# Expert routing inside the attention stage, a ring of eleven weight pieces, and rows added where they belong: a hybrid encoder layer on one core

## Chip, core and metric

The kernel runs on one core of a Trainium2 chip. The metric is the device time of one execution in microseconds, the median over several runs. The kernel before took 1273.96 us (three runs: 1273.96, 1270.16, 1274.58).

## What is computed

One encoder layer is applied to two sequences of 512 tokens of width 1024 that share all weights. The parts after the token mixer are what matters here:

```python
x = x + mix
x = x + memory_cross_attention(rms_norm(x, norm_xa), rms_norm(mem, norm_mem), w_xq, w_xkv, xq_norm, xk_norm, w_xo)
x = x + hier_moe(rms_norm(x, norm_ffn), w_router_group, b_router_group, w_router_expert, b_router_expert,
                 w_e_gate, w_e_up, w_e_down)
...
# hier_moe, for each of the 1024 tokens:
g_sel = argmax(g_logits)                  # 1 of 4 groups, gate = max of the softmax
top_val, top_loc = top_k(e_logits[g_sel], 2)   # 2 of the 8 experts in that group
gates = softmax(top_val) * g_gate
y = sum over the two experts of gate * ((silu(x @ w_e_gate[e]) * (x @ w_e_up[e])) @ w_e_down[e])
```

There are 32 experts; one has 3 MiB of float32 weights (gate and up 1024x256 each, down 256x1024). A block of work is one expert with up to 128 of its tokens. 1024 tokens with two experts each are 64 tokens per expert on average.

## The kernel before

**Arithmetic.** Each float32 product is made from three fast ones (`three`, L832 to L838): ScalarE copies a float32 tile to a rounded high part (L1263), VectorE subtracts it from the original to get the low part (L1992 for expert weights, L1985 for token rows), and TensorE adds high x high, high x low and low x high.

**Stages.** A table of steps (`timeline`, L61) sets one order in which every engine walks through the mixer and the cross-attention. The cross-attention part runs over eight tiles of 128 tokens (L124 to L143); a tile's last step is its router product (`router`), of which VectorE keeps only the logits (L1862). Engines wait for each other by semaphores alone; each executes its own list in order.

**Routing.** After the last router product VectorE makes the choice for all 1024 tokens at once (L1877 to L1960): maxima, one-hot masks, ranks inside an expert (TensorE sums, L1144), slots, and the list of token numbers per expert (`ids`, sixteen small products at L1155). TensorE has nothing else to do there. Meanwhile SyncE loads weights, and ScalarE and GpSimd prepare expert 0 (GpSimd makes its low parts, L2222).

**Experts.** The 32 experts run in a software pipeline (`pipeline`, a hardware loop over pairs). Six buffers `eraw` of 512 KB hold raw pieces of one expert; high and low parts go to further double buffers. For expert n, TensorE transposes the gathered rows of expert n+1 (L1169), makes gate and up for n, then the down product of n-1. GpSimd gathers the rows of expert n+2 from `ffn_rows` by an indirect DMA (L2236, behind a tiny `anchor` operation, L2235), and stores the 128 result rows of expert n-1 to `expert_rows` (L2245). SyncE reloads a raw piece when its low part is made (L806). An indirect DMA skips the list's empty places.

**Combine.** When all 32 are stored, GpSimd fetches for each token tile the two result rows per token (sixteen indirect DMAs, L2288), VectorE adds them with their gates to `x_sb` (L2064), and SyncE writes the outputs (L828). Experts with more than 128 tokens would take `further` blocks; none occurs with these inputs.

Of the kernel before, what the change touches and what calls it, by code (L numbers as in the profile page):

```python
# [17 lines left out]
I32 = mybir.dt.int32  # L18
# [28 lines left out]
NB = NE + NO  # L47
# [4 lines left out]
N_RAW = 2  # L52
N_BANKS = 8
N_FIRST = 2
N_CONST = 8
N_INIT = 8
ROUND = 2.0 ** 23
R_STAGES = 5


def timeline():  # L61
# [62 lines left out]
    for i in range(-2, NT + 2):  # L124
# [38 lines left out]
def bank_uses(step):  # L163

    kind = step[0]
    if kind == "conv" or kind in ("vc", "vt", "dtp", "z", "mv", "hn1", "dt", "sback", "sout", "router", "dtt", "out"):
        return 1
# [108 lines left out]
def encoder_layer(nc, dram, out):  # L276
# [3 lines left out]
    with ctx:  # L280
# [3 lines left out]
        bank = [ctx.enter_context(nc.psum_tensor(f"bank{b}", [P, 512], F32)) for b in range(N_BANKS)]  # L284
# [5 lines left out]
        y_dram = nc.dram_tensor("expert_rows", (NE * P, D), F32).ap()  # L290
        yo_dram = nc.dram_tensor("further_rows", (NO * P, D), F32).ap()


        x_sb = ctx.enter_context(nc.sbuf_tensor("x_sb", [P, NT, D], F32))
        ident = ctx.enter_context(nc.sbuf_tensor("ident", [P, P], F32))
        logits = ctx.enter_context(nc.sbuf_tensor("logits", [P, NT, NG + NE], F32))
        stk = ExitStack()
        ctx.enter_context(stk)

        def sb(name, shape, dt=F32):  # L300
            return stk.enter_context(nc.sbuf_tensor(name, shape, dt))
# [109 lines left out]
        router_w = sb("router_ws", [P, KT, NG + NE])  # L411
        sb("apart", [P, 320])
# [6 lines left out]
        router_b = sb("router_b", [P, NG + NE])  # L419
        stk.close()  # L420
        NORMED = {"mix": (xn, gain), "mem": (xn, gain), "xa": (xn, gain), "ffn": (xn_ffn, gain_ffn)}


        def se(name, shape, dt=F32):
            return ctx.enter_context(nc.sbuf_tensor(name, shape, dt))

        WgH = [se(f"WgH{i}", [P, KT, 2 * DE], F32R) for i in range(2)]
        WgL = [se(f"WgL{i}", [P, KT, 2 * DE], F32R) for i in range(2)]
        WdH = [se(f"WdH{i}", [P, 2, D], F32R) for i in range(2)]
        WdL = [se(f"WdL{i}", [P, 2, D], F32R) for i in range(2)]  # L430
        eraw = [se(f"eraw{j}", [P, 1024]) for j in range(6)]
        xg = [se(f"xg{i}", [P, D]) for i in range(2)]
        xgH = [se(f"xgH{i}", [P, KT, P], F32R) for i in range(2)]
        xgL = [se(f"xgL{i}", [P, KT, P], F32R) for i in range(2)]
        eth = se("eth", [P, DE])
        ehb = se("ehb", [P, DE])
        hbH = se("hbH", [P, 2, P], F32R)
        hbL = se("hbL", [P, 2, P], F32R)
        ey = [se(f"ey{i}", [P, D]) for i in range(2)]
        idc = [se(f"idc{i}", [P, 1], U32) for i in range(2)]  # L440

        iota_e = se("iota_e", [P, NB + 1])
        iota_p = se("iota_p", [P, P])
        token0 = se("token0", [P, NT])
        token1 = se("token1", [P, NT])
        anchor = se("anchor", [P, 1])
        r_g = se("r_g", [P, NT, NG])
        r_g2 = se("r_g2", [P, NT, NG])
        r_e = se("r_e", [P, NT, NE])
        r_eq = se("r_eq", [P, NT, NE])  # L450
        oh = se("oh", [P, 2, NT, NE])
        r_max = se("r_max", [P, 3, NT])
        r_idx = se("r_idx", [P, 3, NT])
        gates = se("gates", [P, 2, NT])
        r_t = se("r_t", [P, 4, NT])
        cnt_b = se("cnt_b", [P, NT, NE], BF16)
# [1904 lines left out]
```

## Time and profile before

| | us |
|---|---|
| median of three runs | 1273.96 |
| span of the profiled execution | 1272.4 |
| last router logits on VectorE | 835.8 |
| first gate/up product of an expert | 887.2 |
| last down product ends | 1221.5 |
| busy: TensorE / VectorE / ScalarE / GpSimd | 1028.0 / 838.4 / 525.7 / 263.0 |

The time of an execution has its span in it and what lies around the span; the profiled execution's own time is not given beside its span, and the median of the runs is 1.6 us above that span. The span falls into a long part under the step table (to 836 us), routing (to 887), the experts (to 1221) and the combine. A timeline row gives start, duration, engine, line, operation and output<-inputs; where it is marked x4, four like instructions in a row are merged.

### The profile page before, as it was taken

The page shows a single profiled execution, that of the slowest core. Times are in us where ns is not written, and L with a number is a line of the kernel's source. Part 1 is how long each engine was busy: PE and PEld are TensorE (multiplying, and loading weights), DVE is VectorE, ACT ScalarE, POOL GpSimd, SP SyncE. Part 2 cuts the span into 40 slices and gives each one's busy share as a digit, 9 for nine tenths or more (in the row PEclk, how much of TensorE's full clock was granted, in tenths as well). Part 3 has the DMA queues.
Part 4 walks back from the last instruction along what each step waited for, and adds up shares of the span by engine and source line. Part 5 has one row for each costly group of instructions (what it writes and reads, how often), then busy time and mean ns, then how long its engine had stood idle before and what let it go on. Part 6 is the DMA issues. An engine that isn't in the chain of part 4 may idle for free. (4 is left out here: it accounts for less than half of the span.)

```text
span 1272.4 us, 15688 instructions
## 1 busy us (share of the span) xinstructions
PE 1028.0 (81%) x5076; PEld 833.5 (66%) x5076; DVE 838.4 (66%) x1295; ACT 525.7 (41%) x944; POOL 263.0 (21%) x364
## 2 busy tenths in 40 slices
PE   1878979988897989899969999822899989999930
PEld 1656757766675768778758788722777777777720
DVE  4425856876675586752445554376899999999934
ACT  3222243323234333321233333231677777777710
POOL 1204304321431331100101111142111111111123
PEclk9989988878898888889979999755999999999975
DMA  5131214122122313424210000053799999999948
GB/s 183 36 97 61 91 67 126 30 72 75 59 91 69 131 59 111 138 80 143 72 50 1 34 17 34 33 180 130 261 382 371 373 373 383 389 363 370 351 139 306
DMA packets 75800, 201.41 MB, mean 158 GB/s; under 512 B 13088, under 2 KB 19648, under 8 KB 75744
## 3 DMA queue, kind: packets, MB, share of 16 engines
q1 hardware_dynamic: 58240, 151.15, 33.5%
q0 software_dynamic: 15808, 47.89, 10.4%
q10 hardware_dynamic: 1696, 1.65, 0.4%
q8 instruction: 32, 0.52, 0.2%
q14 instruction: 24, 0.20, 0.1%
HBM read 177.58 MB, written 31.46 MB: 164 GB/s over the span
## 5 line engine op out<-in xcount | busy, mean ns | idle before, releaser
L836 PE MATMUL bank<-Wh,hTh 128*128 128x512 f32 x384 | 162.0, 422 | 4.6 <-issue 4.6
L837 PE MATMUL bank<-Wl,hTh 128*128 128x512 f32 x384 | 156.8, 408 | 0.0
L838 PE MATMUL bank<-Wh,hTl 128*128 128x512 f32 x384 | 156.1, 407 | 0.0
L1992 DVE TENSOR_TENSOR WgL<-eraw,WgH 128x1024 fp32r<-128x1024 f32 x124 | 143.5, 1216 | 0.6 <-ACT WgH L1263 0.5
L1263 ACT ACTIVATE WgH<-eraw 128x1024 fp32r<-128x1024 f32 x128 | 127.0, 1064 | 12.1 <-DMA eraw<-w_e_up 8.5
L836 PE MATMUL bank<-WgH,xgH 128*128 128x512 f32 x256 | 103.6, 405 | 0.0
L1580 DVE TENSOR_TENSOR Wl<-raw,Wh 128x1024 fp32r<-128x1024 f32 (+1 forms) x64 | 77.3, 1216 | 37.9 <-ACT Wh L1263 37.7
L837 PE MATMUL bank<-WgL,xgH 128*128 128x512 f32 x256 | 100.9, 394 | 0.0
L838 PE MATMUL bank<-WgH,xgL 128*128 128x512 f32 x256 | 100.5, 393 | 0.0
L836 PEld LDWEIGHTS bank<-Wh,hTh 128*128 128x128 f32 x384 | 77.6, 202 | 22.4 <-issue 6.6
L838 PEld LDWEIGHTS bank<-Wh,hTl 128*128 128x128 f32 x384 | 76.3, 199 | 17.3
L837 PEld LDWEIGHTS bank<-Wl,hTh 128*128 128x128 f32 x384 | 77.2, 201 | 15.7
L836 PE MATMUL bank<-hTh,Wh 128*128 128x512 f32 (+1 forms) x176 | 74.3, 422 | 9.2 <-issue 8.3
L1992 DVE TENSOR_TENSOR WdL<-eraw,WdH 128x1024 fp32r<-128x1024 f32 x62 | 73.2, 1220 | 6.7 <-ACT WdH L1263 6.4
L1263 ACT ACTIVATE Wh<-raw 128x1024 fp32r<-128x1024 f32 (+1 forms) x64 | 63.1, 999 | 30.4 <-PE bank L838 19.6
L1263 ACT ACTIVATE WdH<-eraw 128x1024 fp32r<-128x1024 f32 x64 | 64.5, 1050 | 25.3 <-PE bank L838 22.1
L886 PE MATMUL bank<-ident,xn 128*128 128x128 f32 x160 | 31.2, 359 | 52.6 <-DVE xn L1589 52.6
L837 PE MATMUL bank<-hTl,Wh 128*128 128x512 f32 (+1 forms) x176 | 72.7, 413 | 0.0
L838 PE MATMUL bank<-hTh,Wl 128*128 128x512 f32 (+1 forms) x176 | 72.4, 411 | 0.0
L2245 POOL DMA_DIRECT2D expert_rows<-ey x32 | 18.7, 583 | 214.8 <-DVE ey L2016 198.8
L886 PEld LDWEIGHTS bank<-ident,xn 128*128 128x128 f32 x160 | 25.1, 186 | 57.0 <-DVE xn L1589 38.0
L1413 ACT ACTIVATE dec<-dec,ncs 128x128 f32<-128x128 f32 x128 | 38.6, 388 | 45.2 <-DVE dec L1774 45.2
(314 smaller groups left out, 2261.7 us busy)
## 6 DMA issues: line engine op xcount, KB each, us to landing
eraw<-w_e_gate SPq DMA_DIRECT2D x64, 512.0 KB, 6.0
eraw<-w_e_up SPq DMA_DIRECT2D x64, 512.0 KB, 6.5
eraw<-w_e_down SPq DMA_DIRECT2D x64, 512.0 KB, 6.4
raw<-w_in SPq DMA_DIRECT2D x72, 256.0 KB, 2.9
expert_rows<-ey POOLq DMA_DIRECT2D x32, 512.0 KB, 6.4
raw<-w_xkv SPq DMA_DIRECT2D x16, 256.0 KB, 3.0
raw<-w_out SPq DMA_DIRECT2D x16, 256.0 KB, 3.4
raw<-mix_scratch SPq DMA_DIRECT2D x16, 256.0 KB, 3.2
```

Of the source, the lines that this page charges most:

```text
L836: pe.matmul(dst, ah, bh, start=first, stop=False)
L837: pe.matmul(dst, ah, bl, start=False, stop=False)
L838: return pe.matmul(dst, al, bh, start=False, stop=last)
L886: last = pe.transpose(b[:, j * P:(j + 1) * P], NORMED[st][0][:, f * P:(f + 1) * P], ident[:, :])
L1263: return act.activation(dst, src, ACT.Copy, **kw)
L1413: last = act.activation(dec[:, dr, h, :], dec[:, dr, h, :], ACT.Exp, bias=ncs[:, dr, c, h:h + 1])
L1580: tt(lo, src, h, ALU.subtract).then_inc(w_low, 1)
L1992: tt(lo, as_piece(eraw[j], j), h.bitcast(F32), ALU.subtract).then_inc(ew_low, 1)
L2245: pool.dma_start(rows_, ey[i][:, :]).then_inc(ey_st[i], 16)
```

## The change

**Per-tile routing.** Two steps `rank` and `slots` join the table, and the `router` step does the whole choice for its own tile with the eight-largest operations of VectorE. After the last tile only one product (`place`) is left before the token numbers are known. The gates are computed later, beside the first expert.

**Weights.** Eleven buffers of 1 MiB each (three pieces per expert) are laid over memory that the attention stage gives back. The low part is written in place over the raw piece; high parts have three buffers for gate/up and two for down. SyncE issues the first eleven loads from the last attention tiles on, and each further one when TensorE has used the piece. The hardware loops are gone: all 32 experts are written out.

**Rows.** ScalarE stores `x` of each tile to `partial_rows` during attention. For each expert GpSimd gathers the token rows and the partial rows; VectorE adds gate times result to the partial rows; GpSimd scatters them by three indirect DMAs, to `partial_rows` for a token's first expert and to `y_prompt` or `y_sample` for its second (places that do not belong to a target are out of range and skipped). Experts of the four groups alternate, so that neighbours share no token. There is no combine.

**Low parts.** GpSimd makes half of the down piece's low part, a sixth of an expert's.

```diff
     for i in range(-2, NT + 2):
...
+        tl += on(i - 2, ("rank", i - 2), ("slots", i - 2))
...
+        if i == NT:
+            tl.append(("pre",))
...
-    return tl
+    return tl + [("place",)]
...
+                    link(dve.max(gm8[:, i, :], logits[:, i, 0:8]))
+                    link(dve.max_index(gi8[:, i, :], gm8[:, i, :], logits[:, i, 0:8]))
+                    link(dve.tensor_copy(r_ix[:, 0:1], gi8[:, i, 0:1]))
+                    link(ts(r_pen[:, :], iota_e[:, 0:NG], r_ix[:, 0:1], NEG, ALU.not_equal, ALU.mult))
...
+            wait_full(sp, ("hn1", "xq", NT - 1))
+            for q in range(3 * NE):
+                n, j = divmod(q, 3)
...
+                elif q >= N_EW:
+                    m, i = divmod(q - N_EW, 3)
+                    if i < 2:
+                        sp.wait_ge(g_used, 2 * m + i + 1)
+                    else:
+                        sp.wait_ge(d_used, m + 1)
+                load_piece(expert(n), j, q % N_EW, eraw_ld[q % N_EW])
...
+            def gather_rows(n):
+                e = expert(n)
+                if n > 2:
+                    pool.wait_ge(xg_full, 2 * n - 4)
+                fetch(xg[n % 3][:, :], hn_dram, idh[:, e:e + 1], last_row).then_inc(xg_ld[n % 3], 16)
...
+            def store_rows(n):
+                e = expert(n)
+                pool.wait_ge(ey_done, n + 1)
+                done, rows_ = out_st[n % 4], pg[n % 4][:, :]
+                spread_rows(out[0][0], idp[:, e:e + 1], rows_, last_half).then_inc(done, 16)
+                spread_rows(out[1][0], ids[:, e:e + 1], rows_, last_half).then_inc(done, 16)
+                spread_rows(px_dram, idf[:, e:e + 1], rows_, last_row).then_inc(done, 16)
+
+            def down_low(n):
+                k = piece(n, 2)[0]
+                pool.wait_ge(dhi_done, n + 1)
+                pool.tensor_tensor(elo[k][:, D:2 * D], eraw[k][:, D:2 * D], dhi[n % 2][:, 1, :].bitcast(F32),
+                                   ALU.subtract).then_inc(dlo_p, 1)
...
+            for n in range(1, NE):
+                if n > 1:
+                    store_rows(n - 2)
+                if n + 1 < NE:
+                    gather_sums(n + 1)
+                if n + 3 < NE:
+                    gather_rows(n + 3)
+                if n + 1 < NE:
+                    down_low(n + 1)
...
+            def add_rows(n):
+                e = expert(n)
+                dve.wait_ge(d_used, n + 1)
+                dve.wait_ge(pg_ld[n % 4], 16 * (n // 4 + 1))
+                stt(pg[n % 4][:, :], y_ps[:, :], gate_s[:, e:e + 1], pg[n % 4][:, :], ALU.mult, ALU.add)\
+                    .then_inc(ey_done, 1)
...
-            for i in range(NT):
-                for c in range(2):
-                    dve.wait_ge(yg_ld[i % 2][c], 16 * (i // 2 + 1))
-                    stt(x_sb[:, i, :], yg[i % 2][c][:, :], gates[:, c, i:i + 1], x_sb[:, i, :], ALU.mult, ALU.add)\
```

The first place is VectorE in a middle tile of cross-attention. `xn` is the normalised input of a later tile, which TensorE transposes as soon as it is there. Before:

```order
L1862 TENSOR_TENSOR logits<-bank,router_b 128x36
L1589 SCALAR_TENSOR_TENSOR xn<-x_sb,rs,gain 128x1024
L1825 COPY probT<-bank 128x512
L1597 TENSOR_TENSOR hTl<-bank,hTh 128x4x128 x2
L1640 TENSOR_SCALAR xqT<-bank,cols 128x512
```

Now (`eix`, `oh`, `cnt_b` and `idv` are the tile's expert numbers, one-hot masks, counts and token values):

```order
L1989 TENSOR_TENSOR logits<-bank,router_b 128x40
L1991 MAX gm<-logits 128x8
L1992 MAX_INDEX gi<-gm,logits 128x8
L1993 CAST r_ix<-gi 128x1
L1994 TENSOR_SCALAR r_pen<-iota_e,r_ix 128x4
L1995 TENSOR_TENSOR r_e<-logits,r_pen 128x32
L1997 MAX em<-r_e 128x8
L1998 MAX_INDEX ei<-em,r_e 128x8
L1999 CAST eix<-ei 128x2
L2001 TENSOR_SCALAR oh<-iota_e,eix 128x32 x2
L2003 TENSOR_TENSOR cnt_b<-oh 128x32
L2006 TENSOR_TENSOR csum<-csum,cnt_b 128x32
```

Behind these come two more (L2008, `idv`), and only then `xn` (now L1710): fourteen instructions stand between the logits and `xn` where there was none.

The second place is GpSimd among the experts. Before, one expert in the loop is:

```order
L2235 TENSOR_TENSOR anchor<-token 128x1
L2236 DMA xg<-ffn_rows,idc 128x1024
L2243 REGISTER_ALU
L2245 ISA
L2245 DMA expert_rows<-ey 128x1024
```

Now one expert is (`pg` holds partial rows, `elo` the low part over the raw piece):

```order
L2382 DMA y_prompt<-pg_86,idp 512x1024
L2382 DMA y_sample<-pg_86,ids 512x1024
L2382 DMA partial_rows<-pg_86,idf 1024x1024
L2377 DMA pg_89<-partial_rows,idh 128x1024
L2377 DMA xg_85<-ffn_rows,idh 128x1024
L2408 TENSOR_TENSOR elo_63<-eraw_52,dhi_78 128x1024
```

One indirect and one plain DMA have become five indirect ones and an operation on 128x1024 elements.

The third place is VectorE among the experts, one expert of the new order:

```order
L2065 TENSOR_TENSOR hbL<-hb_ps,hbH 128x256
L2046 TENSOR_TENSOR xgL_82<-xg_ps,xgH_80 128x512 x2
L1684 TENSOR_TENSOR elo_72<-eraw_61,ghi_74 128x2048
L1684 TENSOR_TENSOR elo_73<-eraw_62,ghi_75 128x2048
L2059 SCALAR_TENSOR_TENSOR ehb<-eth,gu_ps 128x256
L2061 TENSOR_TENSOR ehb<-ehb,gu_ps 128x256
L2072 SCALAR_TENSOR_TENSOR pg_87<-y_ps,gate_s,pg_87 128x1024
L2052 TENSOR_TENSOR elo_63<-eraw_52,dhi_78 128x1024
```

Six low parts of 1024 columns have become two of 2048 and one of 1024, and the copy of half a result has become an addition over 1024 columns.

## Rows read from the trace of the kernel before

**Rows 1.** Stretches: us, busy PE, PEld, DVE, ACT, POOL (instructions), clock, DMA, GB/s.

```profile
722.00:744.00 22.00, 20.34 (x122) 17.52 (x121) 11.73 (x19) 7.96 (x19) 3.69 (x8) 1.00 0.06 25
...
840.00:880.00 40.00, 2.15 (x32) 1.83 (x32) 33.98 (x59) 12.23 (x13) 19.25 (x10) 0.50 0.52 174
...
960.00:1200.00 240.00, 224.55 (x1061) 182.87 (x1060) 226.19 (x299) 185.00 (x252) 41.73 (x69) 0.99 0.99 375
```

**Rows 2.** Timeline around logits and normalised inputs, tiles 3 and 7 of attention.

```profile
703.59 1.28 DVE L1589 SCALAR_TENSOR_TENSOR xn<-x_sb,rs,gain 128x1024 f32<-128x1024 f32 x1
...
704.92 1.97 PE L886 MATMUL bank<-ident,xn 128*128 128x128 f32 x8 [0.54 <-DVE xn L1589]
...
827.68 0.20 DVE L1862 TENSOR_TENSOR logits<-bank,router_b 128x36 f32<-128x36 f32 x1 [3.40 <-PE bank L1134]
...
829.13 1.97 PE L886 MATMUL bank<-ident,xn_ffn 128*128 128x128 f32 x8 [1.56 <-DVE xn_ffn L1589]
```

**Rows 3.** Timeline from the last logits to the first expert product.

```profile
835.84 0.19 DVE L1862 TENSOR_TENSOR logits<-bank,router_b 128x36 f32<-128x36 f32 x1 [6.78 <-PE bank L1134]
...
846.05 0.17 DVE L1911 TENSOR_SCALAR r_t<-r_t 128x8 f32<-128x8 f32 x1
846.25 0.17 DVE L1912 TENSOR_TENSOR r_t<-r_t 128x8 f32<-128x8 f32 x1
...
870.45 0.82 PE L1155 MATMUL bank<-oneh_b,oneh_p 128*128 128x48 f16 x16 [23.05 <-DVE oneh_b L1954]
...
887.21 0.77 PE L836 MATMUL bank<-WgH,xgH 128*128 128x512 f32 x1
```

**Rows 4.** Groups of instructions, 960 to 1200 us (23 experts).

```profile
L1992 DVE TENSOR_TENSOR WgL<-eraw,WgH 128x1024 fp32r<-128x1024 f32 x92 | 106.4, 1216 | 0.6 <-ACT WgH L1263 0.5
...
L1985 DVE TENSOR_TENSOR xgL<-bank,xgH 128x512 fp32r<-128x512 f32 x46 | 29.4, 679 | 0.1
...
L2236 POOL DMA_INDIRECT xg<-ffn_rows,idc x23 | 24.1, 1048 | 10.8 <-issue 10.8
...
L2001 DVE TENSOR_TENSOR ehb<-ehb,bank 128x256 f32<-128x256 f32 x23 | 9.7, 421 | 0.8
```

**Rows 5.** DMA view, 960 to 1200 us; the second row ends in us to landing.

```profile
DMA packets 26470, 89.95 MB, mean 375 GB/s; under 512 B 4513, under 2 KB 4513, under 8 KB 26470
...
xg<-ffn_rows,idc POOLq DMA_INDIRECT x23, 7.0
```

**Rows 6.** Timeline: down products of the first and last expert, and the combine.

```profile
904.04 0.39 PE L838 MATMUL bank<-WdH,hbL 128*128 128x512 f32 x1
...
1221.09 0.39 PE L838 MATMUL bank<-WdH,hbL 128*128 128x512 f32 x1
...
1230.24 1.03 POOL L2288 DMA_INDIRECT eraw<-expert_rows,slot  x1 [0.30 <-issue]
1231.58 0.99 POOL L2288 DMA_INDIRECT eraw<-expert_rows,slot  x1 [0.30 <-issue]
```

**Rows 7.** Timeline: GpSimd and VectorE side by side, routing and first experts.

```profile
846.34 9.26 POOL L2222 TENSOR_TENSOR WgL<-eraw,WgH 128x1024 fp32r<-128x1024 f32 x4 [7.90 <-ACT WgH L1263]
...
848.76 2.27 DVE L1915 TENSOR_TENSOR gates<-gates,r_t 128x8 f32<-128x8 f32 x1
...
871.92 4.63 DVE L1992 TENSOR_TENSOR WgL<-eraw,WgH 128x1024 fp32r<-128x1024 f32 x4
872.03 1.16 POOL L2235 TENSOR_TENSOR anchor<-token 128x1 f32<-128x1 f32 x1 [11.82 <-DVE idc L1979]
873.36 1.91 POOL L2236 DMA_INDIRECT xg<-ffn_rows,idc  x1 [0.17 <-POOL anchor L2235]
...
992.90 0.18 POOL L2235 TENSOR_TENSOR anchor<-token 128x1 f32<-128x1 f32 x1 [1.65 <-DVE idc L1979]
993.55 1.05 POOL L2236 DMA_INDIRECT xg<-ffn_rows,idc  x1 [0.47 <-issue]
994.11 4.62 DVE L1992 TENSOR_TENSOR WgL<-eraw,WgH 128x1024 fp32r<-128x1024 f32 x4
```

More of the change, by code:

```diff
@@ L421, in encoder_layer @@
+        oh = nc.alloc_sbuf_tensor_at("oh", [P, 2, NT, NE], F32, offset=at["y1"] + 2048)
         NORMED = {"mix": (xn, gain), "mem": (xn, gain), "xa": (xn, gain), "ffn": (xn_ffn, gain_ffn)}
[L424 to L429, printed above, removed]
@@ new lines, in encoder_layer, with sw @@
+        xg = [se("xg0", [P, D], "Wl1", 2 * K4), se("xg1", [P, D], "Wl1", 3 * K4), se("xg2", [P, D], "xn", 4 * K4)]
+        pg = [se(f"pg{i}", [P, D], "xn", K4 * i) for i in range(4)]
+        small = [at["xkT"] + 6 * K4]
+        def sw(name, shape, dt=F32):
+            t = nc.alloc_sbuf_tensor_at(name, shape, dt, offset=small[0])
+            small[0] += -(-int(np.prod(shape[1:])) * 4 // 32) * 32
+            assert small[0] <= at["router_b"]
+            return t
+        eth = sw("eth", [P, DE])
@@ new lines, in encoder_layer, with expert, piece, fill @@
+        out_st = [sem(f"out_st{i}") for i in range(4)]
+        o_v = sem("o_v")
+        o_pe = sem("o_pe")
+        f_id = sem("f_id")
+        f_row = sem("f_row")
+        anchored = sem("anchored")
+        f_ld = [sem(f"f_ld{j}") for j in range(3)]
+        f_v = sem("f_v")
+        f_a = sem("f_a")
+        f_pe = sem("f_pe")
+        def expert(n):
+            return n % NG * EPG + n // NG
+        def piece(n, j):
+            return (3 * n + j) % N_EW, (3 * n + j) // N_EW
+        def fill(n, j):
+            k, turn = piece(n, j)
+            two = sum(x % 3 < 2 for x in range(k, 3 * n + j + 1, N_EW))
+            return eraw_ld[k], 16 * (turn + 1 + two)
@@ L829, in _ @@
-            sp.wait_ge(out_st, 16 * NT)
+                sp.wait_ge(d_used, b + NE)
+                for j in range(3):
+                    load_piece(e, j, j, f_ld[j])
+            further(sp, more, more_first)
         @block.tensor
@@ L1226, in _ @@
-            further(pe, more)
+                last.then_inc(d_used, 1)
+            turn_rows(0)
+            gate_up(0)
+            turn_rows(1)
+            pe.wait_ge(vals_done, 1)
+            for j in range(2 * NT):
+                pe.matmul(r_ps[:, 0:3 * NE].rearrange("p (a b) -> p a b", a=3), oneh_p[:, j, :], idv2[:, j, :, :],
+                          start=j == 0, stop=j == 2 * NT - 1)
+            pe.matmul(r_ps[:, 3 * NE:4 * NE], ones_b[:, :], csum[:, NT, :], start=True, stop=True).then_inc(vals_full, 1)
@@ L1229, in _ @@
+            further(pe, more, more_first)
         @block.scalar
@@ L1522, in _ @@
+            further(act, more, more_first)
         @block.vector
@@ new lines, in _ @@
+            gate_low(0, 1)
+            down_low(0)
+            gate_values()
+            rows_low(0)
+            gate_low(1, 0)
+            hidden(0)
+            rows_low(1)
+            gate_low(1, 1)
+            down_low(1)
+            slot_values()
+            for n in range(1, NE):
+                hidden_low(n - 1)
+                if n + 1 < NE:
+                    rows_low(n + 1)
+                    gate_low(n + 1, 0)
+                    gate_low(n + 1, 1)
+                hidden(n)
+                add_rows(n - 1)
+                if n + 1 < NE:
+                    down_low(n + 1)
+                if n == 2:
+                    counts()
```

973 lines of the change are left out of this document (528 added, 445 removed).

## The prediction
> **What bounds the kernel now.** I read the stretches first [rows 1]. In a tile of cross-attention TensorE is busy 20.3 of 22 us at full clock and VectorE 11.7, so TensorE sets the pace there. From 840 to 880 us TensorE works 2.2 of 40 us: this is routing. Among the experts three things are close to full at once: TensorE 224.6, VectorE 226.2 of 240 us, and the DMA engines at a share of 0.99. The DMA view gives 89.95 MB for 23 experts, 3.91 MB each, at 375 GB/s [rows 5], which is 10.4 us per expert. The timelines fix the stages: last logits at 835.8, first expert product at 887.2 [rows 3], first down product ended at 904.4, last at 1221.5 [rows 6]. So the 31 experts between take 10.23 us each, and 50.9 us follow them up to the span of 1272.4 us. GpSimd is nearly free among the experts: 41.7 us in 240.
>
> **The change, part by part.** All sums run against the span of 1272.4 us; the median of the runs is 1.6 us above it.
>
> *Routing inside attention.* A small dependent VectorE operation follows the one before after 0.20 to 0.21 us [rows 3]. Fourteen of them now stand between a tile's logits and `xn`: 14 x 0.21 = 2.9 us. Before, `xn` began right at the logits, and TensorE already waited for it (0.54 us) [rows 2]. So this is no free time on VectorE: TensorE stands still 2.9 us more in each of the four tiles that still prepare a later one, 11.6 us. In the next two tiles the chain holds up the copy of `probT`; there about half of it shows, 3 us together. Behind the seventh tile's logits stand the chain, the rank product and four operations of `slots`, in front of the last `xn_ffn`, for which TensorE waits [rows 2]: 2.9 + 0.5 + 1.0 = 4.4 us. `slots` also stands ahead of `xn_ffn` in the other tiles, 0 to 1.0 us each; I take 0.6, 3.5 us for six. The small products of `rank` and a clock that may sag with more gaps: 0 to 8 us, I take 3.5. Sum 26 us (bounds 12 and 34), so the last logits come at 862. The forms `MAX` and `MAX_INDEX` are not in this trace; between the smallest operation, 0.17, and one on 256 columns, 0.42 [rows 3, 4], I take the small one, since they read 8 to 40 columns. The stores of `x` by ScalarE and the early weight loads cost nothing: DMA is 0.06 busy there [rows 1].
>
> *From the last logits to the first expert product* it takes 51.4 us now [rows 3]. After the change: the chain 2.9, rank and slots 1.5, sixteen placing products 2.0 (the present ones took 0.82 in half the precision [rows 3]), token numbers 0.5. From `anchor` at 872.0 to the first product at 887.2 were 15.2 us [rows 7, 3]; without `anchor` and the second tile's transposes ahead of the product I take 12. Sum 19 us: the first expert product starts at 881, 6 us earlier only. The first down product ends 17.2 us after that before; now its neighbour's gate/up waits for low parts that TensorE's own use releases, about 3 us more. So it ends at 901 instead of 904.
>
> *An expert in the steady state.* TensorE keeps its work, 224.6/23 = 9.8 us. VectorE: two low parts of 2048 columns and one of 1024 are 5 units of 1.16 us (the step of four in 4.62 [rows 7]), 5.8; token rows 2 x 0.64, three hidden operations of 0.42 [rows 4], the addition 1.3: 9.6 us, from 9.8 now. The DMA volume stays: one full store of 128 rows was as much as a gather and a scatter of 64. The eleven pieces loaded ahead give the queue a lead of about one expert. These three would give 10.3 to 10.7 us per expert.
>
> GpSimd is the new candidate. Two indirect DMAs in a row start 1.34 us apart [rows 6]; five per expert are 6.7. A subtraction over 1024 columns takes 2.31 (9.26 for four [rows 7]). With 0.1 for waits that is 9.1 us in a list that has to be done in order. And it does not get them undisturbed. At 872.0 `anchor` took 1.16 us beside the low parts of VectorE, where it takes 0.18 at 992.9; the indirect DMA behind it took 1.91 instead of 1.05; and VectorE's 8-column product of the gates took 2.27 us beside GpSimd's subtractions [rows 7]. So a GpSimd instruction waits for the running two-input operation of VectorE to end, and the other way round. At 993.6 the indirect DMA had begun before the low parts, and neither suffered: it needs the port only at its start. Hence the wait per GpSimd instruction: the port is VectorE's for 5.8 us of an expert, in pieces of 2.3, 2.3 and 1.2, so an arrival in it waits 1.0 us on average. At a pace T the chance of that is 5.8/T, six arrivals per expert: T = 9.1 + 6 x 5.8/T, which is 12.0 us. An instruction that was just served leaves 1.2 us in which it needs no port, so I take a little less: **T = 11.7**. Its ends: 10.3, where the waits fall on nothing, and 14.9, where GpSimd makes no progress in all of the 5.8 us. An indirect DMA that scatters is not in the trace; between a plain store's 0.58 us of issue and the 1.91 of a hindered gather I take the gather's 1.34.
>
> In return VectorE waits for GpSimd's 2.31 us operation, for none of it or all. The two ask for the port when the same high part is ready, and VectorE has other operations to do in part of that time, so I take a third, 0.8 us: VectorE needs 10.4 us, inside the 10.3 to 10.7.
>
> The Trainium skill, "Perfetto Trace Analysis", section "Optimizing Scalar/DVE Operations", speaks against this part of the change: since GpSimd and VectorE share a read port, moving work between the two might not help. Taken to its end it would give VectorE 9.6 + 2.3 = 11.9 us per expert in place of 10.4; the rows at 848.8 and 872.0 show the port waits it speaks of, and not how much of them lies beside other work.
>
> *Sum.* GpSimd runs up to two experts ahead at the start. Its gather for expert 5 is issued at about 914 (the down product of expert 0 at 901, its addition, three scatters, two gathers with their waits). From there 26 experts at T to the gather of the last one. Behind that: subtraction 3.3, two shorter rounds of 9.1 without the token gather, then the last three result sets at 3 x 1.34 = 4 us each, 12; landing 5.5 (gathers take 7.0 in a full queue [rows 5]) and 2 for the ends of all engines, with 1.3 for the addition: 42 us. 914 + 26 x 11.7 + 42 = 1260, and 1.6 for what lies around: **1262 us**. What the combine cost, 50.9 us, is mostly gained; the slower experts take most of it back.
>
> **Rivals.**
>
> *A, the forecast*: GpSimd sets the pace, T from 11.2 to 12.2: 1249 to 1275. For it speak the two port rows; against it, that the order of arrivals can lock into a phase with few waits. Chance 0.50.
>
> *B, GpSimd keeps up*: then TensorE, VectorE and DMA hold 10.5 us: 901 + 31 x 10.5 + 13 (addition, scatters, landing, end) + 1.6 = 1241; with 10.3 to 10.7, and attention up to 12 us quicker, 1223 to 1248. It needs waits under 1.5 us per expert. Chance 0.30.
>
> *C, slower than before*: the same mechanism, but arrivals fall at the start of the wide operations, as at 872.0, where the two instructions waited 0.98 and 0.9 us of pieces of 1.16. With pieces twice as wide, two such arrivals per expert wait 1.9 us each, even if the other four wait for nothing: T = 9.1 + 3.8 = 12.9, and 914 + 26 x 12.9 + 42 + 1.6 = 1293. It decides from T = 12.4 on. It also comes about if a scatter costs 0.4 us more than a gather. Chance 0.17.
>
> *D, GpSimd is shut out wholly*: its pace is 9.1 + 5.8 = 14.9, the time 1345 us. The gather at 993.6 that ran on in 1.05 us beside four low parts speaks against it; 0.03. The page "SBUF — State Buffer" of the Trainium skill, section "SBUF: two separate sides", says that GpSimd cannot write the descriptors of its DMAs while VectorE is in an operation that takes both ports. If a two-input subtraction counted as such a one, this case would be the rule.
>
> **How the numbers follow.** A measurement of this kernel can tell 0.5% from no change, 6.4 us: faster is below 1267.6, slower above 1280.3. A lies below 1267.6 in 6 of 10, between in 3.5: 0.30 and 0.17, the rest 0.03 above. B is faster, 0.30. C and D are slower, 0.20. Faster 0.60, same 0.17, slower 0.23. The range takes in A, the upper two thirds of B and C: 1225 to 1293. The likeliest case's own range is 1249 to 1275.
>
> **What would show it.** Last logits near 862 and TensorE's wait for `xn` near 3.5 us instead of 0.54; first expert product near 881. Among the experts: GpSimd without idle time except its port waits, indirect DMAs longer than 1.05 us on average (near 1.5), TensorE waiting for `xg`, DMA share near 0.85. If instead indirect DMAs are near 1.05 and GpSimd waits for VectorE's additions, B holds. If the last logits stay near 836, my first term is wrong, and the time is 26 us lower in every case.

## The result, and the profile after

The changed kernel takes **1293.09 us** (median of 4 runs, 1290.03 to 1294.7), the kernel before 1272.06 us beside it (1269.9 to 1274.58). The ratio is 1.0167, with a 95% interval of 1.0147 to 1.0186: slower by 1.7%. The forecast was 1262 us, faster. The profiled execution took 1290.03 us, with a span of 1288.2.

The stretches of the changed kernel, to be laid beside [rows 1] (same columns):

```profile
722.00:744.00 22.00, 17.42 (x97) 15.35 (x96) 12.85 (x35) 5.51 (x13) 3.31 (x7) 0.84 0.11 44
840.00:880.00 40.00, 19.94 (x100) 17.31 (x98) 24.35 (x70) 12.03 (x14) 14.51 (x18) 0.61 0.34 119
960.00:1200.00 240.00, 206.46 (x892) 167.14 (x891) 199.60 (x173) 141.45 (x135) 212.95 (x116) 0.92 0.88 320
```

In attention TensorE does less in the same time, at a lower granted clock (0.84, where it had 1.00; among the traced kernels with this attention code, 0.77 to 0.92 in that window). Among the experts TensorE and VectorE have both become less busy, and GpSimd went from 41.7 to 213 of 240 us. What its six instructions per expert cost is in the groups of that stretch (mean ns; then the idle time ahead of them and its releasers):

```profile
L2382 POOL DMA_INDIRECT y_prompt<-pg,idp x20 | 53.9, 2696 | 3.3 <-issue 3.2
L2408 POOL TENSOR_TENSOR elo<-eraw,dhi 128x1024 fp32r<-128x1024 f32 x20 | 50.5, 2527 | 0.5
L2382 POOL DMA_INDIRECT y_sample<-pg,ids x19 | 37.7, 1985 | 5.8 <-issue 5.8
L2377 POOL DMA_INDIRECT pg<-partial_rows,idh x19 | 25.5, 1341 | 5.8 <-issue 5.8
L2382 POOL DMA_INDIRECT partial_rows<-pg,idf x19 | 23.6, 1239 | 5.8 <-issue 5.8
L2377 POOL DMA_INDIRECT xg<-ffn_rows,idh x19 | 22.3, 1176 | 5.8 <-issue 4.3 <-PE xg_ps L1222 1.5
```

The six means add up to 10.96 us, and the issue gaps (0.3 us ahead of an indirect DMA, 0.17 behind the subtraction) bring them to 12.4. Of the idle time only 1.5 us in 240 are a wait for another engine: GpSimd's list is full. TensorE in its turn waits for the row gathers that GpSimd issues, as the longest waits of the same stretch show (in total, times, longest):

```profile
ACT dhi L1354 <- PE y_ps L897: 44.1, 18, 2.5
PEld xg_ps L1222 <- DMA xg<-ffn_rows,idh: 21.5, 16, 2.7
DVE elo L1684 <- ACT ghi L1354: 19.5, 26, 1.7
PEld hb_ps L1247 <- DVE ehb L2061: 18.5, 10, 2.9
PE xg_ps L1222 <- DMA xg<-ffn_rows,idh: 18.5, 16, 2.5
```

**Where the time went**, by the end of the twelve down products of the first and of the last expert. Now they end at 903.9 and 1275.2 us, before at 904.4 and 1221.5 [rows 6]. The way to the first is 0.5 us shorter. The 31 experts between take 11.98 us each instead of 10.23: 54.3 us more. Behind the last it takes 13.0 us to the span's end instead of 50.9: 38.0 less. Together -0.5 + 54.3 - 38.0 = +15.8, the difference of the spans (1288.2 - 1272.4). So scattering partial rows did save the closing combine, and slower experts took more than that back.

One round of GpSimd (POOL) and of VectorE (DVE) shows how. These are rows of the timeline of the changed kernel: start, duration, then in brackets the idle time ahead.

```profile
1045.90 2.42 POOL L2408 TENSOR_TENSOR elo<-eraw,dhi 128x1024 fp32r<-128x1024 f32 x1
1048.48 2.88 POOL L2382 DMA_INDIRECT y_prompt<-pg,idp  x1 [0.17 <-issue]
1051.67 2.39 POOL L2382 DMA_INDIRECT y_sample<-pg,ids  x1 [0.30 <-issue]
1054.37 0.98 POOL L2382 DMA_INDIRECT partial_rows<-pg,idf  x1 [0.31 <-issue]
1055.65 1.03 POOL L2377 DMA_INDIRECT pg<-partial_rows,idh  x1 [0.30 <-issue]
1056.99 1.56 POOL L2377 DMA_INDIRECT xg<-ffn_rows,idh  x1 [0.31 <-PE xg_ps L1222]
1058.57 2.42 POOL L2408 TENSOR_TENSOR elo<-eraw,dhi 128x1024 fp32r<-128x1024 f32 x1
1061.15 2.88 POOL L2382 DMA_INDIRECT y_prompt<-pg,idp  x1 [0.17 <-issue]
```

```profile
1047.75 2.72 DVE L1684 TENSOR_TENSOR elo<-eraw,ghi 128x2048 fp32r<-128x2048 f32 x1 [1.11 <-ACT ghi L1354]
1050.90 2.29 DVE L1684 TENSOR_TENSOR elo<-eraw,ghi 128x2048 fp32r<-128x2048 f32 x1 [0.42 <-ACT ghi L1354]
...
1056.43 1.23 DVE L2052 TENSOR_TENSOR elo<-eraw,dhi 128x1024 fp32r<-128x1024 f32 x1 [0.72 <-ACT dhi L1354]
...
1059.66 5.69 DVE L1684 TENSOR_TENSOR elo<-eraw,ghi 128x2048 fp32r<-128x2048 f32 x2 [0.47 <-ACT ghi L1354]
```

VectorE's first wide low part (2048 columns) begins in the last half microsecond of GpSimd's subtraction, and waits for its end (2.72 us, where the next takes 2.29). The scatter to `y_prompt` then meets that operation from its start and ends 0.89 us after it (1051.36 against 1050.47). The scatter to `y_sample` starts 0.8 us into the second and ends 0.87 us after it. The row gather meets the low part of 1024 columns and ends 0.89 us after that. The two that fall between, at 1054.37 and 1055.65, take 0.98 and 1.03. The next subtraction ends at 1060.99. VectorE's next wide operation was ready at 1059.66 and is held until then (the two records together last 5.69 us, where twice 2.29 is 4.6), and the next `y_prompt` takes 2.88 us again.

That is what keeps the two lists in step. In 17 of the 19 rounds from 960 to 1200 us a wide operation becomes ready while the subtraction runs, 0.4 to 2.5 us before its end. It is held to that end, and `y_prompt`, which starts 0.17 us behind the subtraction, meets it at its start: 2.88 us each time. In the other two rounds no wide operation becomes ready in that time, and `y_prompt` takes 1.02 us.

### The profile page after: what moved, and what is told of

Same layout as the page of the kernel before. It is cut to its first block and busy times, and to the rows that moved or that the text cites. A ratio compares the mean times of both kernels' runs of the same rounds, so it can differ in the third digit from the quotient of the medians.

```text
span 1288.2 us, 14286 instructions
## 1 busy us (share of the span) xinstructions
PE 1065.4 (83%) x5093; PEld 863.5 (67%) x5093; DVE 842.8 (65%) x1285; ACT 501.3 (39%) x816; POOL 519.3 (40%) x445
## 5 line engine op out<-in xcount | busy, mean ns | idle before, releaser
L1684 DVE TENSOR_TENSOR elo<-eraw,ghi 128x2048 fp32r<-128x2048 f32 x64 | 173.0, 2727 | 26.5 <-ACT ghi L1354 25.7
L1354 ACT ACTIVATE ghi<-eraw 128x2048 fp32r<-128x2048 f32 x64 | 121.7, 1918 | 21.6 <-PE gu_ps L897 19.5
L895 PE MATMUL gu_ps<-ghi,xgH 128*128 128x512 f32 x256 | 111.8, 437 | 5.7 <-DVE xgL L2046 5.7
L896 PE MATMUL gu_ps<-elo,xgH 128*128 128x512 f32 x256 | 106.3, 415 | 0.0
L897 PE MATMUL gu_ps<-ghi,xgL 128*128 128x512 f32 x256 | 105.5, 412 | 0.0
L1354 ACT ACTIVATE dhi<-eraw 128x2048 fp32r<-128x2048 f32 x32 | 61.2, 1912 | 75.6 <-PE y_ps L897 73.1
L2408 POOL TENSOR_TENSOR elo<-eraw,dhi 128x1024 fp32r<-128x1024 f32 x32 | 82.0, 2562 | 15.4 <-ACT dhi L1354 14.7
L2233 POOL TENSOR_SCALAR hms<-hss 128x4 f32<-128x4 f32 (+1 forms) x20 | 3.9, 194 | 195.7 <-DVE hss L1726 195.6
L2382 POOL DMA_INDIRECT y_prompt<-pg,idp x32 | 78.8, 2463 | 7.3 <-issue 4.9
L2233 POOL TENSOR_SCALAR ms<-ssq 128x1 f32<-128x1 f32 x28 | 5.4, 194 | 185.5 <-ACT xn L1410 145.2
```

The costliest lines, as they stand in the source:

```text
L895: pe.matmul(dst, ah, bh, start=first, stop=False)
L896: pe.matmul(dst, ah, bl, start=False, stop=False)
L897: return pe.matmul(dst, al, bh, start=False, stop=last)
L1354: return act.activation(dst, src, ACT.Copy, **kw)
L1684: tt(elo[k][:, :], eraw[k][:, :], ghi[g % 3][:, :, :, :].rearrange("p a k n -> p (a k n)").bitcast(F32), ALU.subtract).then_inc(glo_done, 1)
L2233: link(pool.tensor_scalar(tmp, src, scale, eps, ALU.mult, ALU.add))
```

## Experiments

| kernel | us, median (range, runs) | ratio to before, 95% | first down product begins | us per expert |
|---|---|---|---|---|
| before | 1272.06 (1269.9 to 1274.58) | | 901.5 | 10.23 |
| changed | 1293.09 (1290.03 to 1294.7, 4) | 1.0147 to 1.0186 | 900.9 | 11.98 |
| e1_no_gpsimd_low | 1267.49 (1263.76 to 1270.42, 10) | 0.9938 to 0.9982 | 898.4 | 11.3 |
| e2_low_in_1024 | 1279.23 (1270.96 to 1283.14, 10) | 1.0024 to 1.0078 | 904.0 | 11.5 |
| e3_choice_later | 1270.88 (1267.06 to 1272.07, 10) | 0.9966 to 0.9999 | 879.5 | 12.0 |
| e4_one_scatter | 1257.25 (1251.8 to 1260.06, 4) | 0.985 to 0.9917 | 904.6 | 10.6 |
| e5_all_three | 1237.97 (1237.06 to 1239.8, 4) | 0.9708 to 0.9766 | 880.3 | 11.0 |
| e6_late_no_low | 1239.60 (1234.91 to 1243.04, 4) | 0.9703 to 0.977 | 875.3 | 11.3 |
| e7_low_ahead_of_gather | 1371.28 (1368.44 to 1374.26, 4) | 1.0758 to 1.0826 | 901.2 | 14.5 |
| e8_ring_of_8 | 1294.43 (1290.59 to 1295.66, 4) | 1.0153 to 1.0213 | 901.0 | 12.0 |
| e9_late_no_low_one_scatter | 1228.89 (1224.67 to 1229.55, 4) | 0.964 to 0.9712 | 877.8 | 10.7 |

The last column is the time from the end of the first expert's down products to the end of the last one's, in the profiled execution, over 31. Each ratio is to runs of the kernel before that were made beside that kernel; their median was 1272.1 us for the changed kernel, 1273.1 for e1 to e4, 1271.2 for e5 to e8 and 1268.3 for e9. Gains of a few us between kernels that were not run together are therefore rough.

### No low halves on GpSimd

```diff
-                tt(elo[k][:, 0:D], eraw[k][:, 0:D], dhi[n % 2][:, 0, :].bitcast(F32), ALU.subtract).then_inc(dlo_v, 1)
+                tt(elo[k][:, :], eraw[k][:, :], dhi[n % 2][:, :, :].rearrange("p k n -> p (k n)").bitcast(F32),
+                   ALU.subtract).then_inc(dlo_v, 1)
...
-                if n + 1 < NE:
-                    down_low(n + 1)
```

> VectorE makes the whole low part of the down piece, GpSimd none. Theory (GpSimd's list and its waits for the port set the pace of 12.6 us per expert): GpSimd loses 2.5 us of work and the blocking of VectorE by it, about 8.8 us with its waits; then VectorE leads with 6 x 1.16 + 1.3 + 1.26 + 1.3 = 10.8 us, so 10.8 to 11.2 per expert and 1293 - 31 x 1.6 = 1243 (1235 to 1255). Rival 1 (VectorE or TensorE sets the pace in the changed kernel): VectorE has 1.2 us more, 13 us per expert or more, 1300 and above. Rival 2 (the landing of gathered rows under DMA load): no change, 1290.

It gained 25.6 us, half of the 50 that was expected. The expectation set out from 12.6 us for an expert, where the changed kernel takes 11.98 over all of them. And two waits came in place of the full list, as the waits from 960 to 1200 us show:

```profile
POOL y_prompt L2382 <- DVE pg L2072: 21.8, 15, 4.3
POOL pg L2377 <- DMA partial_rows<-pg,idf: 20.7, 11, 2.8
PE xg_ps L1222 <- DMA xg<-ffn_rows,idh: 21.5, 16, 2.2
```

GpSimd now waits for others, so its list is no longer the limit, yet an expert takes 11.3 us and not 10.5. The five indirect DMAs still take 8.15 us in place of five times 1.0 (means 1594, 1807, 1375, 1909 and 1462 ns): the 3.1 us of port waits are spread over all five once nothing holds them in step.

### Narrower operations on VectorE

```diff
-                tt(elo[k][:, :], eraw[k][:, :], ghi[g % 3][:, :, :, :].rearrange("p a k n -> p (a k n)").bitcast(F32),
-                   ALU.subtract).then_inc(glo_done, 1)
+                for c in (slice(0, 1024), slice(1024, 2048)):
+                    ins = tt(elo[k][:, c], eraw[k][:, c],
+                             ghi[g % 3][:, :, :, :].rearrange("p a k n -> p (a k n)")[:, c].bitcast(F32), ALU.subtract)
+                ins.then_inc(glo_done, 1)
```

> The two gate/up low parts of 2048 columns are made as four of 1024; nothing else changes, VectorE has 0.1 us more work per expert. Theory of port waits (a GpSimd instruction waits for the running VectorE operation): y_prompt falls from 2.7 to about 1.7 us, y_sample from 2.0 to about 1.6, sum of the waits from 3.7 to 2.3 us per expert, 11.2 per expert, 1293 - 28 x 1.4 = 1254 (1245 to 1270). Rival (the first scatter is dear in itself): y_prompt stays at 2.7, the time at 1293 to 1296.

The groups on GpSimd:

```profile
L2384 POOL DMA_INDIRECT y_sample<-pg,ids x20 | 35.6, 1782 | 6.1 <-issue 6.1
L2384 POOL DMA_INDIRECT y_prompt<-pg,idp x21 | 33.4, 1589 | 3.4 <-issue 3.1
...
L2410 POOL TENSOR_TENSOR elo<-eraw,dhi 128x1024 fp32r<-128x1024 f32 x21 | 57.8, 2752 | 16.7 <-ACT dhi L1354 16.3
```

The same work in halves takes 1.1 us off the scatter to `y_prompt` (2696 to 1589 ns): a waiting instruction gets in at the end of the running operation, so the operation's width sets the price. The port theory holds in kind: the rival said that `y_prompt` would stay at 2.7. The total fell by 14 us only, less than expected; the subtraction now waits for ScalarE's high part (16.3 us in 240).

### The choice of experts behind the transposes

The operations between a tile's logits and its rank product become a step `pick` of their own, listed behind the last attention step's transposes and `xn`:

```diff
+        if i < NT:
+            tl += on(i - 2, ("pick", i - 2))
...
-        tl += on(i - 2, ("rank", i - 2), ("slots", i - 2))
+        if i < NT:
+            tl += on(i - 2, ("rank", i - 2), ("slots", i - 2))
+        if i > NT:
+            tl += [("pick", i - 2), ("rank", i - 2), ("slots", i - 2)]
```

> The fourteen VectorE operations of a tile's choice stand behind xqT, in front of oTl, instead of in front of xn (for the seventh tile behind the last xn_ffn). Theory (they held TensorE up, and its clock fell in the gap): a middle tile takes 22.5 to 23.5 us instead of 27.3, the last logits come at 838 to 845 instead of 861, and the time falls by 16 to 23 us, to 1273 (1268 to 1279). Rival (the chain costs the same wherever it stands, since VectorE is needed later in the tile): under 8 us gained.

It gained 22.2 us. The last logits come at 839.4 instead of 861.3, and TensorE is busy for 21.1 of 22 us again:

```profile
722.00:744.00 22.00, 21.10 (x118) 18.33 (x118) 13.90 (x37) 8.09 (x19) 3.31 (x7) 0.92 0.12 49
```

The experts are as before the edit, at 12.0 us each (`y_prompt` 2794 ns). So the cost in attention was not the work, which VectorE still does there, but its place ahead of `xn`.

### Without the scatters to the outputs

The two scatters to `y_prompt` and `y_sample` are left out, and nothing is written to the outputs.

```diff
-                spread_rows(out[0][0], idp[:, e:e + 1], rows_, last_half).then_inc(done, 16)
-                spread_rows(out[1][0], ids[:, e:e + 1], rows_, last_half).then_inc(done, 16)
```

> The scatters to y_prompt and y_sample are left out, so the outputs are not written; the scatter to partial_rows, both gathers and GpSimd's subtraction stay. Theory: GpSimd has 2.53 + 3 x 1.3 + 1 of waits, 7.5 us per expert, and TensorE and VectorE lead with 10.4 to 10.8: 1293 - 31 x 2.0 - 3 = 1228 (1220 to 1240). Rival (VectorE, slowed by the port, sets the pace): 12 us per expert, above 1275.

The groups on GpSimd:

```profile
L2406 POOL TENSOR_TENSOR elo<-eraw,dhi 128x1024 fp32r<-128x1024 f32 x23 | 75.0, 3259 | 19.3 <-ACT dhi L1354 17.8 <-issue 1.1
L2382 POOL DMA_INDIRECT partial_rows<-pg,idf x23 | 62.1, 2699 | 3.7 <-issue 3.1
L2377 POOL DMA_INDIRECT pg<-partial_rows,idh x22 | 39.1, 1779 | 6.7 <-issue 6.7
```

`partial_rows`, third behind the subtraction and 1239 ns in the changed kernel, is now first behind it and takes 2699 ns, what `y_prompt` took there. So 2.7 us is the price of that place, not of that scatter. The two scatters less saved 36 us instead of the 65 expected: their waits passed to what stands around them (the partial-row gather went from 1341 to 1779 ns, the subtraction from 2527 to 3259), and TensorE is nearly full then, 223.9 of 240 us.

### The subtraction between the scatters and the gathers

```diff
                 if n > 1:
                     store_rows(n - 2)
                 if n + 1 < NE:
+                    down_low(n + 1)
                     gather_sums(n + 1)
                 if n + 3 < NE:
                     gather_rows(n + 3)
-                if n + 1 < NE:
-                    down_low(n + 1)
```

> GpSimd makes its low half behind the three scatters and ahead of the two gathers, instead of behind the gathers; nothing else differs from the changed kernel. Theory (what is dear is the place behind the subtraction, because the subtraction ends when VectorE begins the two wide operations, and each indirect DMA that starts while one of them runs ends 0.87 us after it): the partial-row gather and the row gather become the dear ones (2.3 to 2.8 us and 1.8 to 2.2), the scatter to y_prompt falls to 1.0 to 1.6, the sum of a round stays at 10.5 to 11.5, the time 1285 to 1300. Rival (arrivals are random with respect to VectorE's operations, so each kind has its own price): y_prompt stays at 2.4 to 2.8 us and the gathers at 1.2 to 1.4.

The durations went the way of the theory: `y_prompt` fell from 2696 to 1017 ns, and the gather that now stands behind the subtraction is the dearest indirect DMA, at 1972. Both gathers stayed below the ranges given (the row gather took 1413), perhaps because VectorE has less to do at this pace. The time did not go that way; it is 78 us above the changed kernel, and I had not seen why it would be. The groups and the waits from 960 to 1200 us:

```profile
L2408 POOL TENSOR_TENSOR elo<-eraw,dhi 128x1024 fp32r<-128x1024 f32 x16 | 46.4, 2903 | 70.0 <-ACT dhi L1354 69.9
L2377 POOL DMA_INDIRECT pg<-partial_rows,idh x16 | 31.6, 1972 | 2.5 <-issue 2.2
...
L2382 POOL DMA_INDIRECT y_prompt<-pg,idp x15 | 15.3, 1017 | 4.6 <-issue 4.6
```

```profile
ACT xgH L1354 <- PE xg_ps L1222: 71.9, 16, 9.9
POOL elo L2408 <- ACT dhi L1354: 69.9, 8, 9.6
...
PE xg_ps L1222 <- DMA xg<-ffn_rows,idh: 64.2, 8, 9.1
```

Every second round GpSimd stands some 9 us at the subtraction, waiting for ScalarE's `dhi`. ScalarE has `xgH` ahead of that in its list and waits for TensorE's transposes, and TensorE for a row gather that is queued behind the subtraction. Moving one instruction ahead of two closed a loop of waits over three engines. It is no deadlock, since the rows are gathered two rounds ahead, but the round trip sets the pace.

### A shorter ring

The three pieces in the place of `xkT` are left out, and the three waits that guarded them.

> A ring of 8 weight pieces instead of 11, all in places that are free before the expert loop. Theory (GpSimd's list sets the pace, weights are there in time): the time stays within 5 us of the changed kernel, 1288 to 1298, and no wait for a weight piece above 5 us in the window from 960 to 1200. Rival (the depth of the ring carries the loop, since the DMA engines are 85 to 95% busy): ACT's rounding waits for pieces, 1305 us or more.

1294.43 us, 1.3 more than with eleven: no difference. The waits for weight pieces are ScalarE's, 15.7 us (for `w_e_up`, 11 times) and 4.6 us (for `w_e_down`, 3 times). The first is three times the bound given, and both cost nothing while GpSimd's list is the longest. The ring's depth is neither the loss nor a gain here.

### Both undoings together

> The two undoings together, e3 and e1: choice of experts later, no low halves on GpSimd. Theory (the losses lie in different stretches and add up: 22 us in the attention, 25.6 us in the expert loop): 1293 - 22.2 - 25.6 = 1245 us (1241 to 1251), faster than the kernel before by 2%; last logits at 839, first expert product at 872, the expert loop as in e1 (PE 212 us busy of 240). Rival (an earlier start of the expert loop is lost again later, because transfers have less lead): 1255 us or more, with PE's waits for weights or rows above those of e1.

1239.6 us: the two gains (22.2 and 25.6) add up, to 1293.1 - 47.8 = 1245, and another 6 us were gained, whose cause I do not know. The expert loop is that of e1. The 872 us given for the first product was a misreading of mine: it belongs to the second expert in e3, whose first expert starts at 860.1; here it is 857.5. **This kernel is 2.6% faster than the one before** (2.3 to 3.0%), so the rest of the change, with the choice placed later, does pay.

### The row gather ahead of the scatters

On top of the last one:

```diff
             for n in range(1, NE):
+                if n + 3 < NE:
+                    gather_rows(n + 3)
                 if n > 1:
                     store_rows(n - 2)
                 if n + 1 < NE:
                     gather_sums(n + 1)
-                if n + 3 < NE:
-                    gather_rows(n + 3)
```

> Three edits together: the choice of experts moved behind the transposes of the attention's last step (as in e3), no low halves on GpSimd (as in e1), and GpSimd issues an expert's row gather ahead of the scatters and the partial-row gather of its round. Theory (what still holds the expert loop of e1 is that row gathers stand behind a wait for the landing of scattered partial rows and come late: 21.5 us of PE's waits in 240): the waits for xg fall to under 8 us, PE's busy time in the window from 960 to 1200 us rises from 212 to about 222, an expert takes 10.6 us instead of 11.2, and the time is about 1230 us (1225 to 1240), 13 to 18 us below e6_late_no_low. Rival (the DMA engines, 94% busy in e1, are the bound, and a row gather lands late wherever it is issued): the same time as e6_late_no_low within 5 us, and the row gathers' landing times grow by what they are issued earlier.

TensorE's waits for `xg` went away as planned, and the time is the same (1237.97 against 1239.60, ranges that overlap). An expert takes 0.3 us less in the profiled execution, and the loop starts 5 us later; the last logits are already 5 us later there (841.6 against 836.7), in a part that the edit does not touch. Other waits took their place:

```profile
POOL pg L2387 <- DMA partial_rows<-pg,idf: 35.6, 19, 4.3
ACT ghi L1361 <- DMA eraw<-w_e_up: 33.3, 17, 3.4
PE hb_ps L1255 <- DVE ehb L2071: 27.4, 21, 2.7
```

Now the landing of partial rows and the weights are late. The rival gave the time rightly, and the DMA engines are at 0.94. Its reason is only half borne out: a row gather lands as fast as before (14.2 and 14.4 us in the median), and it is the down pieces that land later, 21.2 us instead of 14.0.

### Both undoings, without the scatters to the outputs

Here too the outputs are not written.

> e6_late_no_low with the scatters to y_prompt and y_sample left out (the outputs are not written), so that GpSimd issues 3 indirect DMAs per expert instead of 5, 256 small descriptors fewer. In e6 the DMA engines are 93% busy, 20.7% of it with the indirect DMAs, an expert takes 11.3 us and GpSimd is busy for 172 of 240 us. Theory (the DMA engines with their many small packets now bound the expert loop): the two scatters carry 40% of the indirect DMAs' packets and some 16% of their bytes, 3 to 8% of the engines' time, so an expert takes 10.4 to 10.9 us and the time is about 1224 us (1216 to 1232); the waits for row gathers fall below 10 us of 240. Rival (the bound is the chain over TensorE, ScalarE and VectorE, with TensorE busy for 213 of 240 us at a clock of 0.95): 1234 us or more, with the DMA engines' share down to 0.88.

The time is 10.7 us below that of e6, in the upper part of the theory's range. By the ratios to the kernel before it is 7.6 us; the two were not run together. The waits for row gathers are gone. What the DMA engines did is best read from 960 to 1180 us, since e9 issues its last weight load at 1179 us. These are the columns of [rows 1] and the packets of [rows 5] for that stretch, first of the kernel before, then of e6, then of e9:

```profile
960.00:1180.00 220.00, 205.46 (x971) 167.41 (x970) 207.03 (x274) 169.48 (x232) 38.20 (x63) 0.99 0.99 374
DMA packets 24145, 82.25 MB, mean 374 GB/s; under 512 B 4069, under 2 KB 4069, under 8 KB 24145
```

```profile
960.00:1180.00 220.00, 195.49 (x874) 158.06 (x874) 195.16 (x172) 139.54 (x134) 159.56 (x96) 0.95 0.93 343
DMA packets 27488, 75.46 MB, mean 343 GB/s; under 512 B 11541, under 2 KB 11541, under 8 KB 25039
```

```profile
960.00:1180.00 220.00, 197.45 (x935) 159.31 (x934) 206.38 (x184) 147.90 (x142) 108.30 (x60) 0.99 0.95 351
DMA packets 23496, 77.28 MB, mean 351 GB/s; under 512 B 7244, under 2 KB 7244, under 8 KB 20903
```

Share times 220 us, over the MB moved, is the time that one MB kept the engines busy: 2.65, 2.71 and 2.70 us. An expert has 3.15 MB of weights and on average 192 rows of 4 KB (128 stored and 64 gathered before, 128 gathered and 64 scattered now), 160 in e9: 3.93 MB before and in e6, 3.80 in e9. That makes, as an estimate, 10.4 us of the DMA engines per expert before, 10.7 in e6 and 10.3 in e9. The bytes of an expert did not grow, but the small packets did, from some 195 to 600 per expert. The five indirect DMAs go through 5 x 128 places and find 192 rows; before it was 128 places and 64 rows. That is 384 skipped places more per expert, and some 400 packets of 4 bytes more were counted. In e9 (three indirect DMAs, 160 rows) the same sum gives 160 more than before, and some 160 more were counted.

The estimates lie close to the paces, 11.3 in e6 and 10.7 in e9, and in e9 ScalarE waits for a `w_e_up` piece 23 times (24.8 us in 240). TensorE is busy for 197 of the 220 us there, at 0.99 of the clock. Which of the two holds e9, and what ends e6's last 0.6 us over 10.7, is not settled.

## Why the prediction failed, step by step

**Attention, +26 us: right in sum, not in its parts.** The last logits came at 861.25 (forecast 862). The wait is as forecast: TensorE waited 4.02, 3.68, 2.84 and 2.83 us for `xn` in the four middle tiles, where 0.54 + 2.9 = 3.4 was forecast, and from the first `MAX8` to the start of `xn` it is 2.92 us:

```profile
730.61 0.17 DVE L1991 MAX8 gm<-logits 128x8 f32<-128x8 f32 x1
...
733.15 0.17 DVE L2006 TENSOR_TENSOR csum<-csum,cnt_b 128x32 bf16<-128x32 bf16 x1
...
733.53 1.28 DVE L1710 SCALAR_TENSOR_TENSOR xn<-x_sb,rs,gain 128x1024 f32<-128x1024 f32 x1
...
734.87 1.54 PE L945 MATMUL bank<-ident,xn 128*128 128x128 f32 x6 [3.68 <-DVE xn L1710]
```

The new forms `MAX8` and `FIND_INDEX8` take 0.16 to 0.20 us, the small end, as taken. The term of the clock was too small. From the logits of one middle tile to those of the fourth after it (columns of [rows 1]), before and now:

```profile
703.50:791.40 87.90, 82.16 (x467) 71.27 (x465) 45.72 (x69) 31.04 (x74) 12.46 (x26) 0.96 0.06 25
```

```profile
703.70:812.30 108.60, 91.61 (x471) 78.93 (x470) 59.46 (x151) 31.26 (x74) 12.45 (x26) 0.84 0.16 58
```

Of the 20.7 us more, 11.6 are waits for `xn` (1.8 before, 13.4 now; forecast 11.6). Another 9.4 are TensorE's own busy time for the same products, at a granted clock of 0.84 in place of 0.96; I had 3.5 us for the clock and the small products in all tiles together. The last three tiles took 4.5 us more, where I had 7.4 for the chain and for what stands around it, and some of the 3.5 us of `slots`. So it is luck that the errors cancel. e3 shows the cause by itself: 22.2 us come back with the place, and the same four tiles take 92.0 us at a clock of 0.93.

**From the logits to the first down product: right within 3 us.** The first expert product starts at 881.97 (881). From the last logits to it are 20.7 us, where 19 was forecast, and the sixteen placing products account for that: they took 3.60 us, at a granted clock of 0.50, instead of 2.0. The first expert's down products end at 903.9 (901): they come 21.9 us behind its first product instead of 20.2.

**GpSimd's pace: this step failed.** By its own three terms, from the row gather of expert 5 (918.35, forecast 914) over 26 rounds to the gather of the last one (1241.65), and the 46.6 us behind it (42):

- the start 4.3 us late, of which 2.9 are the first down product,
- a round of (1241.65 - 918.35)/26 = 12.43 us instead of 11.7: 19 us,
- the end 4.6 us longer: its two shorter rounds took 10.8 us each, with the same waits in them, instead of 9.1.

Together 28 us, which is the miss (a span of 1288.2 against 1260). The term inside the round that was mis-sized is the waits. The base was 8.7 (five times 1.0, 2.31, and 1.4 of gaps) where I had 9.1; the waits are 12.4 - 8.7 = 3.7 us where I took 2.6. The arrivals do not fall at random: 1.7 of the 3.7 us lie on `y_prompt` and 1.0 on `y_sample`, at the same place of every round. TensorE waits for a row gather in 16 of 19 rounds (18.5 us), and VectorE's wide operations come behind TensorE's transposes and ScalarE's high parts, so both run at the pace of GpSimd's list. What fixes the distance is the port itself: a wide operation that becomes ready during the subtraction is held to its end, in 17 of 19 rounds, and the next instruction of GpSimd meets it from its start. The one after that starts well into the second wide operation and waits 1.0 us on average. My formula let only GpSimd's instructions arrive at random, and left out that its own subtraction decides when VectorE's operations begin. That is rival C's mechanism, with its place; e4 and e7 show that the price moves with the place, e2 that it falls with the width. C's own price was 3.8 us of waits, and it was to decide from T = 12.4: that is where T came out. That C's time, 1293 us, is the measured one is luck: it put a round at 12.9, and with 12.43 its sum gives 1281; the late start and the longer end add 9 us, and the profiled execution lies 3 us below the median. I gave C 0.17 and had already written down the row that speaks for it, 1.91 us behind an operation met at its start [rows 7].

Also against me: without the deduction for instructions just served, my formula gave 12.0, which would have been 1270 us. Where GpSimd has slack (e1), five arrivals at random would wait 5 x 7.0/11.3 x 1.1 = 3.4 us, and 3.1 were measured. So the formula is sound for engines that are not in step, and wrong for a list that runs at the rhythm of the engine it waits for.

**VectorE: right.** It was not the bound. Its wide low parts took 2794 ns on average in the changed kernel and 2285 in e1, 0.5 us each, 1.0 per expert where I had 0.8. The rule on the shared port (the Trainium skill, "Perfetto Trace Analysis", section "Optimizing Scalar/DVE Operations") is borne out by e1: without that move the kernel is 25.6 us faster. (Not all of that is the port, since GpSimd's list is also 2.4 us of work shorter then.) The page "SBUF — State Buffer" of the Trainium skill, section "SBUF: two separate sides", says of an operation in a 2-port mode that GpSimd cannot write descriptors while it runs. Had that held for these two-input subtractions, a round would have taken 14.9 us by my estimate for D; it is 12.4. An indirect DMA that has begun runs on beside a two-input subtraction, as the `pg` gather did at 1055.65 (1.03 us, with VectorE's subtraction from 1056.43). By a count over the ten traces from 900 to 1270 us, none of 316 indirect DMAs behind whose start a low part began 0.2 us or more later took longer than 1.04 us, and VectorE's operation was not longer either (2.28 to 2.29 us for the wide ones in the median).

**The saved combine: right in kind.** 38.0 us came off the end. Of the signs named beforehand, TensorE's waits for `xg` are there, the DMA share is 0.88 (0.85), and an indirect DMA takes 1.69 us on average (1.5).

Not tried: a kernel in which only the phase of the two lists differs. Each edit that moved it (e4, e7) moved other things as well. The two rounds of the changed kernel in which `y_prompt` met no wide operation are the nearest thing to it.

## What to carry to other kernels

An in-order list that is full, and whose engine shares a port with its neighbour, has no random arrivals here. Its long operation holds the neighbour's back and lets it go at its own end, so the instruction behind the long operation is the one to price at nearly the full width of the neighbour's operation (1.9 of 2.3 us here), every round. Before work is handed to an engine that "is free", add up its new list per round, waits included, and compare it with the pace of the bound engine: here it was 8.7 us without waits against 10.2, and the margin of 1.5 us was less than the waits. And a short dependent chain in the middle of a full stretch costs what it delays: 2.9 us of small operations per tile cost 22 us ahead of `xn`, about half of it in waits and the rest in a lower granted clock. Behind it, the last logits are 3.6 us later than before (0.9 to 5.8 in the four kernels that have it there).

## What I had not expected of the hardware

- An indirect DMA of GpSimd that meets a two-input VectorE operation ends 0.87 to 0.90 us after that operation ends, whatever its length (the middle eight tenths of 81 cases in the changed kernel; both of its operands are in SBUF), and takes 0.97 to 1.04 undisturbed; scatters and gathers cost the same.
- VectorE operations that read one operand from PSUM do not hinder GpSimd: none of 147 indirect DMAs that started beside one (`pg`, `xgL`, `ehb` and `hbL`, in the ten traces) took longer than 1.04 us, and the subtraction at 1058.57 took 2.42 us beside `xgL` (until 1059.19), against 2.31 [rows 7].
- Places that an indirect DMA skips are not free for the DMA engines: a skipped place goes with one packet of 4 bytes, whose record lasts 9 ns on average. The 400 more of them per expert, over 16 engines, are 0.2 us of the some 0.3 us that an expert of e6 keeps these engines busy beyond one of the kernel before, for the same bytes.
- The sixteen placing products, behind a stretch of small work, ran at the lower of the two clocks (1.2 GHz; 3.60 us), and so did the first ten expert products (0.63 us each, then 0.39). The granted clock was 0.50 from 861 to 882 us, where TensorE had only these sixteen, eight transposes (1.95 us) and a few rank products to do, and 1.00 from 888 us on.
